# Latent attention: the causal mask added in VectorE's maximum pass, and TensorE's scores of unit w + 2 issued ahead of the turn of unit w

## The reference, cut to what matters

```
s = jnp.einsum('bhqd,bhkd->bhqk', q_blk, k).astype(jnp.float32) * scale
qpos = i * Q_BLOCK + jnp.arange(Q_BLOCK)
s = jnp.where(kpos[None, :] <= qpos[:, None], s, neg)
p = jax.nn.softmax(s, axis=-1).astype(v.dtype)
return jnp.einsum('bhqk,bhkd->bhqd', p, v)
```

## Time and profile before

| | |
|---|---|
| three runs, median | 1805.03 us (1804.6 to 1806.43) |
| profiled execution: span, first to last instruction | 1807.1 us |
| TensorE busy | 1759.0 us, 97% of the span |
| VectorE busy | 1087.8 us, 60% |
| ScalarE busy | 698.0 us, 39% |
| GpSimd busy | 982.2 us, 54% |

### The profile page before, as it was taken

One profiled execution on the slowest core, in us unless ns is written; L12 is line 12 of the kernel. 1 busy time (PEld: TensorE's weight loads), 2 busy tenths in 40 slices (PEclk: granted clock), 3 DMA queues, 4 the chain that ended last, 5 costly groups with the idle time before them and its releaser, 6 DMA issues.

```text
span 1807.1 us, 25034 instructions
## 1 busy us (share of the span) xinstructions
PE 1759.0 (97%) x8599; PEld 1467.8 (81%) x8599; DVE 1087.8 (60%) x1535; ACT 698.0 (39%) x1243; POOL 982.2 (54%) x554
## 2 busy tenths in 40 slices
PE   7999999999999899999999999999999999999998
PEld 7888888888888677788878888778888888878887
DVE  5655663002334778884345564887777777889842
ACT  7422223111013667731133232644444444444432
POOL 6743333445654577654433232577777777655540
PEclk9999999999999999999999999999999999999999
DMA  6511111347661789583221134243433334494322
GB/s 266 204 52 36 36 43 49 139 164 256 227 227 46 276 317 325 177 308 113 103 71 59 59 104 141 77 139 107 142 117 123 133 110 139 142 344 143 122 76 93
DMA packets 111245, 262.33 MB, mean 145 GB/s; under 512 B 7744, under 2 KB 50368, under 8 KB 106688
## 3 DMA queue, kind: packets, MB, share of 16 engines
q1 hardware_dynamic: 84720, 182.13, 30.3%
q10 hardware_dynamic: 26448, 79.18, 11.8%
HBM read 186.82 MB, written 73.92 MB: 144 GB/s over the span
## 4 chain that ended last, share of the span: by engine, by line
PE 84%; DVE 6%; ACT 5%; issue 2%; DMA 1%; POOL 1%; ACTq 0%; DVEq 0%; SPq 0%; POOLq 0%
PE ps L714 16%; PE ps L719 16%; PE ps L720 16%; PE ps L1333 7%; PE ps L1338 7%; PE ps L1335 7%; PE ps L1408 2%; PE ps L1409 2%; PE ps L1410 2%; ACT prow L1792 2%; PE ps L1110 1%; PE ps L1090 1%; DMA raw<-in_slabs 1%; DVE aneg L2570 1%; PE ps L1431 1%
## 5 line engine op out<-in xcount | busy, mean ns | idle before, releaser
L609 POOL TENSOR_SCALAR wh<-raw 128x1024 fp32r<-128x1024 f32 x75 | 211.6, 2822 | 467.3 <-PE ps L714 448.9
L714 PE MATMUL ps<-uh,wh 128*128 128x512 f32 x560 | 221.2, 395 | 0.7 <-POOL wl L602 0.7
L720 PE MATMUL ps<-uh,wl 128*128 128x512 f32 x560 | 218.4, 390 | 0.0
L719 PE MATMUL ps<-ul,wh 128*128 128x512 f32 x560 | 218.0, 389 | 0.0
L611 POOL TENSOR_TENSOR wl<-raw,wh 128x1024 fp32r<-128x1024 f32 x75 | 182.0, 2427 | 6.3
L646 POOL TENSOR_TENSOR wl<-raw,wh 128x512 fp32r<-128x512 f32 x88 | 137.5, 1573 | 69.1 <-ACT wh L1457 67.8
L633 POOL TENSOR_TENSOR over_rings<-over_rings 128x512 f32<-128x512 f32 x92 | 118.2, 1285 | 51.5 <-DMA over_rings<-in_slabs 45.9
L1457 ACT ACTIVATE wh<-raw 128x512 fp32r<-128x512 f32 (+1 forms) x164 | 105.4, 656 | 88.9 <-PE ps L1338 58.0
L689 POOL TENSOR_TENSOR wl<-raw,wh 128x512 fp32r<-128x512 f32 x63 | 93.7, 1496 | 78.2 <-ACT wh L1457 78.2
L2212 DVE SCALAR_TENSOR_TENSOR ya<-zA,sm,ya 128x512 f32<-128x512 f32 x88 | 109.6, 1246 | 31.7 <-ACT ya L2036 24.6
L720 PEld LDWEIGHTS ps<-uh,wl 128*128 128x128 f32 x560 | 105.1, 188 | 22.6
(11 more groups left out here) (488 smaller groups left out, 4873.9 us busy)
## 6 DMA issues: line engine op xcount, KB each, us to landing
raw<-in_slabs SPq DMA_DIRECT2D x110, 512.0 KB, 3.6
over_rings<-in_slabs SPq DMA_DIRECT2D x22, 1024.0 KB, 7.1
s_s<-over_rings SPq DMA_DIRECT2D x22, 1024.0 KB, 4.9
ssm<-s_s SPq DMA_DIRECT2D x22, 512.0 KB, 4.5
raw<-s_s SPq DMA_DIRECT2D x22, 512.0 KB, 3.8
s_f<-yb ACTq DMA_DIRECT2D x22, 512.0 KB, 5.3
raw<-s_d SPq DMA_DIRECT2D x36, 256.0 KB, 2.5
dsum<-in_slabs SPq DMA_DIRECT2D x16, 512.0 KB, 6.7
```

Source lines behind the costliest of these rows:

```text
L609: pool.tensor_scalar(wh[:, j, :], raw[:, j % RAWS, :], 1.0, None, ALU.mult).then_inc(S["w_hi"], 1)
L714: l = pe.matmul(o, lh, rh, start=start, stop=False)
L719: pe.matmul(o, lh, rl, start=False, stop=False)
L720: return pe.matmul(o, ll, rh, start=False, stop=stop)
```

## The change

VectorE's pass over a unit's scores becomes one `tensor_tensor_reduce`: it reads the scores from PSUM and a mask row `maskt` from SBUF (zeros, and the 128 columns of the diagonal block at its end), writes minus their sum into `prow`, and leaves the least of these, minus the maximum, in `aneg`. ScalarE's exponential reads `prow` (scale -1) and writes it in place. The mask's matmul is gone. As no one reads the banks after VectorE's pass, the scores of w + 2 wait for the maximum of w, not for its exponential, and they are issued ahead of the turn of w. The pass waits for the turn of w - 2, which frees its row buffer. The probabilities' tiles are packed closer (the diagonal blocks at a pitch of 384 columns), which makes room for `maskt`; it is set up by a memset of 896 columns and a copy of 128. The two 128-column copies that made the mask's operands at the kernel's start are gone. Semaphore counts follow.

```diff
             def m_scores(w):
-                at_least(pe, S["m_exp"], w - 1)
+                at_least(pe, S["m_neg"], w - 1)
...
-                    def mask(o=ps[:, bank, n - P:n]):
-                        pe.matmul(o, ident_r[:, :], mask_r[:, :], start=False, stop=False, skip_group_check=True)
                     l = mm3(ps[:, bank, 0:n], mqh[0:QK, i // CH, q], mql[0:QK, i // CH, q], kh[0:QK, keys],
-                            kl[0:QK, keys], True, True, extra=mask if diag else None)
+                            kl[0:QK, keys], True, True)
...
             for w in range(NW):
                 h, r = divmod(w, NT)
+                if w + 2 < NW:
+                    m_scores(w + 2)
                 m_turn(w)
...
-                if w + 2 < NW:
-                    m_scores(w + 2)
...
             def m_exp(w):
-                if w >= 2:
-                    act.wait_ge(S["m_ptt"], PIECE0[w - 1])
-                act.activation(prow[:, w % 2, 0:n], s2(w)[:, 0:n], ACT.Exp,
+                act.activation(prow[:, w % 2, 0:n], prow[:, w % 2, 0:n], ACT.Exp, scale=-1.0,
...
+            dve.memset(maskt[:, 0:T - P], 0.0).then_inc(S["o_z"], 1)
...
             def m_max(w):
-                dve.tensor_reduce(aneg[:, 0, w % 4:w % 4 + 1], ps[:, c:c + 2, :].rearrange("p a n -> p (a n)")[:, 0:n], AX.X,
-                                  ALU.max, negate=True).then_inc(S["m_neg"], 1)
+                if w >= 2:
+                    dve.wait_ge(S["m_ptt"], PIECE0[w - 1])
+                dve.tensor_tensor_reduce(
+                    prow[:, w % 2, 0:n], ps[:, c:c + 2, :].rearrange("p a n -> p (a n)")[:, 0:n], maskt[:, T - n:T],
+                    -1.0, 3e38, ALU.add, ALU.min, aneg[:, 0, w % 4:w % 4 + 1]).then_inc(S["m_neg"], 1)
...
+            dve.tensor_copy(maskt[:, T - P:T], cn[:, CN0["mask"]:CN0["mask"] + P]).then_inc(S["o_z"], 1)
+            dve.wait_ge(S["o_z"], 2)
             m_max(0)
```

More of the change, by code:

```diff
@@ L65, with turned_at, turned_block @@
 PV_PARTS = 3
+DIAG = 3 * P
+def turned_at(t, b, n, i):
+    rows = min(CH * (n + 1), i + 1) - CH * n
+    q = i % CH * P
+    if n < b:
+        return t[:, 0:CH * H2].rearrange("p (a n) -> p a n", n=H2)[:, :, q:q + P]
+    each = t[:, CH * H2 * b:CH * H2 * b + 5 * DIAG].rearrange("p (a n) -> p a n", n=DIAG)
+    return each[:, 1:1 + rows, 0:P] if q == DIAG else each[:, 0:rows, q:q + P]
+def turned_block(t, b, c, q):
+    at = c * H2 if c < CH * b else CH * H2 * b + (c - CH * b) * DIAG
+    return t[:, at + q:at + H2]
 THIRD = (0, 6, 7)
@@ L249, in build @@
         ones_r = sb("ones_r", [P, P], f32r)
-        ident_r = sb("ident_r", [P, P], f32r)
-        mask_r = sb("mask_r", [P, P], f32r)
         posi = sb("posi", [P, NT], i32)
@@ L258, in build @@
         amax, aneg, asum, ainv = (sb(n, [P, 2, CH]) for n in ("amax", "aneg", "asum", "ainv"))
-        sb("line_up_tiles", [P, 80])
+        sb("line_up_tiles", [P, 336])
         ps = ctx.enter_context(nc.psum_tensor("ps", [P, 8, H2], f32))
@@ L290, in build @@
                                              ("qr2", [P, MH, ROPE], 0)])
[L291 to L294, removed]
+        mqh, mql, p0h = place(64, [("mqh", [P, 2, H2], 1), ("mql", [P, 2, H2], 1), ("p0h", [P, 5 * DIAG], 1)])
+        (p0l,) = place(56, [("p0l", [P, 5 * DIAG], 1)])
+        oT, prow, p1h = place(104, [("oT", [P, RH, T], 0), ("prow", [P, 2, T], 0), ("p1h", [P, CH * H2 + 5 * DIAG], 1)])
+        (p1l,) = place(142.5, [("p1l", [P, CH * H2 + 5 * DIAG], 1)])
+        (maskt,) = place(157, [("maskt", [P, T], 0)])
         oth, otl = place(32, [("oth", [P, RH, T], 1), ("otl", [P, RH, T], 1)])
@@ L1073, in m_scores @@
                     bank = 2 + 2 * (w % 2) + c
-                    diag = c == i // CH
                     keys = slice(c * H2, c * H2 + n)
-                    def mask(o=ps[:, bank, n - P:n]):
-                        pe.matmul(o, ident_r[:, :], mask_r[:, :], start=False, stop=False, skip_group_check=True)
                     l = mm3(ps[:, bank, 0:n], mqh[0:QK, i // CH, q], mql[0:QK, i // CH, q], kh[0:QK, keys],
-                            kl[0:QK, keys], True, True, extra=mask if diag else None)
+                            kl[0:QK, keys], True, True)
                 l.then_inc(S["m_s"], 1)
@@ L1108, in m_pv @@
                     c, p = each[k]
-                    qs = slice(max(0, c - CH * b) * P, H2)
-                    l = pe.matmul(ps[:, 1, qs], vr[:, c, h, :, :].rearrange("p a n -> p (a n)"), p[:, c, qs],
+                    q = max(0, c - CH * b) * P
+                    l = pe.matmul(ps[:, 1, q:H2], vr[:, c, h, :, :].rearrange("p a n -> p (a n)"), turned_block(p, b, c, q),
                                   start=k == 0, stop=k == len(each) - 1, skip_group_check=True)
@@ L1129, in mix_first @@
                         pe.wait_ge(S["w_ready"], SLAB0["mix"] + 1)
-                    pe.wait_ge(S["m_exp"], NW - 1 + m)
+                    pe.wait_ge(S["m_neg"], NW - 1 + m)
                     pe.wait_ge(S["o_lo"], 4)
@@ L1778, in o_hi @@
                 copy(oth[:, fb, half(b)], oT[:, fb, half(b)]).then_inc(S["o_hi"], 1)
-            def s2(w):
-                c = 2 + 2 * (w % 2)
-                return ps[:, c:c + 2, :].rearrange("p a n -> p (a n)")
             def m_exp(w):
@@ L1802, in m_pth @@
                     act.wait_ge(S["m_ptt"], q + 1)
-                    copy((p1h if g % 2 else p0h)[:, c0:c1, i % CH * P:(i % CH + 1) * P],
+                    copy(turned_at(p1h if g % 2 else p0h, g % 2, n, i),
                          ps[:, BANK_OF["turn", q], 0:(c1 - c0) * P].rearrange("p (a n) -> p a n", n=P)).then_inc(
@@ L2225, in _ @@
                               inv[:, R64:NF].unsqueeze(1).to_broadcast([P, NT, R16]), ALU.mult).then_inc(S["angs"], 1)
-            for o, n in ((ones_r, "ones"), (ident_r, "ident"), (mask_r, "mask")):
-                dve.tensor_copy(o[:, :], cn[:, CN0[n]:CN0[n] + P]).then_inc(S["cst"], 1)
+            dve.tensor_copy(ones_r[:, :], cn[:, CN0["ones"]:CN0["ones"] + P]).then_inc(S["cst"], 1)
             def angle(n):
@@ L2233, in angle @@
                     dve.tensor_copy(icol[:, :], ps[:, 3, 0:1]).then_inc(S["cst"], 1)
-                    dve.wait_ge(S["cst"], 8)
+                    dve.wait_ge(S["cst"], 6)
                     l = dve.tensor_scalar(ang[:, 0:H2], ps[:, 2, :], icol[:, 0:1], None, ALU.mult)
@@ L2270, in decays @@
                 dve.reciprocal(hx[:, 0, :], xi).then_inc(S["cst"], 1)
-                dve.wait_ge(S["cst"], 10)
+                dve.wait_ge(S["cst"], 8)
                 stt(hx[:, 0, :], hx[:, 0, :], cnc("eps"), hx[:, 0, :], ALU.mult, ALU.mult).then_inc(S["cst"], 1)
@@ L2577, in m_ptl @@
                     c0, c1 = CH * n, min(CH * (n + 1), i + 1)
-                    at = (slice(None), slice(c0, c1), slice(i % CH * P, (i % CH + 1) * P))
                     dve.wait_ge(S["m_pth"], q + 1)
-                    lo((p1l if g % 2 else p0l)[at],
+                    lo(turned_at(p1l if g % 2 else p0l, g % 2, n, i),
                        ps[:, BANK_OF["turn", q], 0:(c1 - c0) * P].rearrange("p (a n) -> p a n", n=P),
-                       (p1h if g % 2 else p0h)[at]).then_inc(S["m_ptl"], 1)
+                       turned_at(p1h if g % 2 else p0h, g % 2, n, i)).then_inc(S["m_ptl"], 1)
             def m_inv(g):
@@ L2685, in clear @@
                 dve.memset(acc_[:, :, :], 0.0).then_inc(S["o_z"], 1)
-                dve.wait_ge(S["o_z"], n + 1)
+                dve.wait_ge(S["o_z"], n + 3)
             def g1_lo(n, h_, gh, gl, gname):
@@ L2843, in _ @@
             dve.memset(zA[:, 0:2], 0.0).then_inc(S["cst"], 1)
-            dve.wait_ge(S["cst"], 12)
+            dve.wait_ge(S["cst"], 10)
             def u_two(i, e):
@@ L2979, in _ @@
             dve.memset(zB[:, 0:2], 0.0).then_inc(S["cst"], 1)
-            dve.wait_ge(S["cst"], 13)
+            dve.wait_ge(S["cst"], 11)
             quarters(0, 0)
```

## The result

The changed kernel takes 1832.87 us, median of 4 runs (1831.58 to 1835.17), against 1804.86 for the kernel before in the same comparison (1804.6 to 1806.43): a ratio of 1.0154, interval 1.0142 to 1.0166. It is slower by 28.0 us, where 16.4 was forecast; 1832.87 lies 2.9 us above the range. The profiled execution spans 1830.4 us, against 1807.1.

What follows compares the result with a forecast made beforehand. No engine bounds the attention throughout: TensorE sets the pace from r0 to r3, ScalarE from r3 on. Terms of 3.8 + 10.0 + 1.4 + 1.2 = 16.4 on 1805.0 gave 1821.4 us, range 1811 to 1830.

Steps and rivals of the forecast that it cites:

- The new wait ahead of the turn of r6: Next head's first scores wait for its queries ahead of r6's turn: 1.43 us in each of 7 heads, 10.0 us.
- rival C: The turn of r6 does not wait, as the chip's order lets it pass: 1811.4 us, chance 0.08.
- what follows the delay: TensorE behind its idle time at r6, forecast at about 1 us: no clock term, so no size given.
- r0 to r3: TensorE's stretch between these turns in heads 1 to 7: 0.54 us longer each as scores move, 3.8 us in all.
- The exponential from SBUF: ScalarE's exponential reads SBUF, not PSUM: 0.034 us more each, about 40 of 64 on the path, 1.4 us.
- The maximum: VectorE's pass with two operands and a written row: 0.062 us more each, 20 of 64 on the path, 1.2 us.
- rival D: VectorE's new pass over the scores streams at half the rate, 2.1 us a head: 1838 us, chance 0.08.
- Set-up: Copies and memset ahead of the attention, two copies gone: taken as 0, ends -0.5 and 1.2 us.

Runs made afterwards that it cites:

- with the idle time filled: Changed kernel plus eight 512-column matmuls that nothing reads, ahead of the wait for the next head's queries: 1822.86 us, ratio 1.0093.
- The mask alone: Changed kernel with all scores made behind the turn, as before; VectorE still adds the mask: 1806.76 us, ratio 1.0006.
- the swap of VectorE's order: Kernel before, with VectorE's maximum of w + 2 ahead of the low part of the next head's keys or queries: 1803.85 us, ratio 0.9994.
- the group at r0 alone ahead, and the maximum first: Changed kernel, only r2's scores ahead of a turn (r0's), maximum of w + 2 ahead of the keys' or queries' low part: 1800.58 us, ratio 0.9976.
- the wait alone: Kernel before, with the turn of r6 also waiting for the low part of the next head's queries: 1810.51 us, ratio 1.0029.
- earlier queries: Changed kernel with three of the four query and key parts made one or two turns earlier: 1817.54 us, ratio 1.0058.
- next head's groups behind the turn: Changed kernel with the scores of a new head's first unit put back behind the turn of r6: 1816.34 us, ratio 1.0057.

## Why the prediction was right in direction and wrong in size

- **The new wait ahead of the turn of r6, delay.** Right. Forecast: 1.60 later, 1.43 net. Measured: 1.72 later in head 3; with the idle time filled, 1.65 later and 0.26 given back by r6 to r7 (2.54 against 2.80), 1.39 net. The forecast followed head 3 alone; in the heads where keys are made the delay is longer, 1.86 to 2.12 with the idle time filled. Over heads 0 to 6 that is 12.6 later, 2.1 given back and 10.6 net, where 10.0 was forecast. That a turn doesn't pass waiting scores (rival C's question) is shown by the rows: in all seven heads the turn came behind them. The rule of the Trainium skill cited there agrees with this trace.
- **The same term, what follows the delay.** This is the step that failed. It priced the wait as lateness alone and named who would wait for the turn, but asked nothing of TensorE itself: what the clock does behind the idle time stood at nothing, without a reason. It put the idle time at about 1 us. That was too small by its own rows: the scores of r7 had stood between the turns of r5 and r6, and with them moved ahead of the turn of r5 that step holds only transposes and values, which end at 694.28 (694.00 + 0.28); from there to 696.54 it is empty. Beside each of the seven gaps the granted clock fell to 0.50 for a few us. The price is the difference that filling makes, 10.0 us. The hint was in the trace of before, 0.58 and 0.57 at 602 to 606 us; the prediction read only the mean of the stage, 0.99.
- **r0 to r3.** Right in kind, a little small: 0.60 to 0.64 in heads 1, 3, 5 and 7, forecast 0.54; in heads 2, 4 and 6, where keys are made too, 0.65 to 1.15. Over heads 1 to 7 it is 5.1 us, forecast 3.8, above its upper end of 4.5. The forecast had taken head 3's 6.43 for all seven heads.
- **The exponential from SBUF.** 39 ns more at 1024 columns, forecast 34.
- **The maximum.** The forecast took a longer pass (62 ns) and held an instruction for the accumulator for the upper end. It is the other way round: the pass isn't longer, and the instruction is there, at 80 ns and not 210. The Trainium skill's rule of two instructions is borne out; rival D, a pass at half the rate, is not. The mask alone shows that the matmuls that went nearly pay for both passes, 2.6 us in the sum: heads 0 to 6 take 150.77 us there, against 150.27 before.
- **Set-up.** Counted at 0; the first turn came 0.65 us later, within its ends. One execution can't tell: in the swap of VectorE's order, which has no new set-up, it came 1.58 later.

By turn distances, the kernel with the idle time filled, which has every term of the sum and not the clock, is 15.25 us longer than before over heads 0 to 6; the sum was 16.4. Its median, 1822.86, stands against the forecast of 1821.4. That they lie so close is in part luck: over these heads r0 to r3 is 5.9 longer where 3.8 was forecast, and the delay 10.6 where 10.0 was, while r3 to r5 and r7 to the next r0, where the sum's 2.6 for the two passes would lie, are 1.2 shorter. The range stopped at 1830 because each upper end was that of a term in the list, and the missing term had none.

Open: how much idle time brings the lower clock; why the time at half clock was twice as long in head 4 as in the six others (there the clock fell before the gap had ended, 0.50 at 722 to 724 us); and whether the fall at the start can be avoided.

## What to carry to other kernels

Price a new wait on TensorE twice: by who gets its result later, and by how long TensorE stands empty, counting the work that the same change moves out of that step; then look in the trace of before for a place where it stood empty and read the clock behind it, in short stretches, since a stage's mean hides it. Work moved ahead of a critical step brings all of its own waits with it, so move only what has been ready for long: here the kernel with the group at r0 alone ahead, and the maximum first, was 4 us faster than the one before, and that with all eight 28 us slower. Where an order changes only in part, look at the seams, where two pieces of work fall into one step.

## What was not expected of the hardware

Idle time of TensorE of 2.26 us (head 3; up to 2.5) was followed by half its clock, seven times of seven, and adding 2.00 us of matmuls that nothing reads made the kernel faster by 10.0 us. Idle time of 1.00 us in the wait alone, and of 1.31 us, was not followed by it. No length of a single gap parts the two: 1.56 us was followed by it and 1.83 us was not (earlier queries, heads 4 and 2), and two gaps of 1.42 and 1.25 us in one step were followed by it in head 4 and not in head 2 (next head's groups behind the turn). VectorE's pass that adds a mask row, writes the sum and keeps the maximum takes 1213 ns for 1024 columns, as long as the plain reduce, 1.21 us.
